# Cross-attention of a decoder block: weights multiplied with the memory once, ahead of the blocks, instead of query, score and value products in every block; six weight slots

## The chip, the cores and the metric

One core of a Trainium2 chip runs the whole step as one program. The metric is device time in microseconds (us) of one execution. Three runs of the kernel before gave 2971.23, 2973.12 and 2975.67 us, median 2973.12. Names: PE is TensorE, DVE VectorE, ACT ScalarE, POOL GpSimd, SP SyncE.

## The reference

The step has 2048 prompt tokens and 8 decode tokens (one each of 8 sequences), all of width 1024. In the order of the reference, with everything in 32-bit floats:

```
h = h + hybrid_mixer(rmsnorm(h, g_mix))              # gated conv and mLSTM, w_in, w_out
kk, vv = split(rmsnorm(mem, g_mem) @ w_xkv)          # 256 memory rows, 4 heads of 256
q = rmsnorm(h, g_cross) @ w_xq                       # per head:
p = softmax(q @ kk.T * 256**-0.5)
h = h + concat(p @ vv) @ w_xo
h = h + (silu(g) * u) @ w_down                       # g, u = split(rmsnorm(h, g_ffn) @ w_gu)
y = rmsnorm(h, g_final)
```

The prompt tokens attend to the 256 new memory rows, which are the same for all of them; each decode token attends to its own cached keys and values (`cache_mem_k`, `cache_mem_v`). The keys and values of the new memory are outputs too.

## The kernel before, in words

Activations are kept with the feature on the partition: a tile holds 8 slices of 128 features, and tokens run along the columns. The 2048 prompt tokens are worked in 5 blocks of 512, 384, 384, 384 and 384 tokens (`BLK`); a block goes through the mixer, the cross-attention and the FFN before the next one begins. The 8 decode columns ride along as columns 385 to 392: in the mixer of block 1 (`DM`), in the output product and the queries of block 2 (`DO`), and in the attention output and the FFN of block 3 (`DX`).

A product with a weight is made of "groups": one group is 128 output features, 8 slices of input, and three passes for each slice (high part of the weight with high and low part of the activation, low part of the weight with the high part), so 24 matmuls of as many columns as the block has tokens; `gemm`, line 518. A group's weight is one tile of 128 by 1024. It needs two forms, high and low (`w_hl`, a slot of 1 MB), of which there are `NS = 5` slots. In a program there are first 16 groups for keys and values (`G_KV`) on 256 columns, then 5 times 121 groups: gate 1, sigmoid gates 4, heads 24, output 8 (`O_OUT`), queries 8 (`O_XQ`), attention output 8 (`O_XO`), FFN 68.

Weights of the first 16 groups and of block 0 arrive unsplit: SP loads 512 KB into one of `NR = 2` raw slots (line 326), ACT copies the high part (`w_high`, line 823), and the low part is subtracted by DVE (first 16 groups, line 1175) or POOL (block 0, line 419); only then SP loads the next weight into that raw slot. In block 0 SP also stores the split weight (line 341), and blocks 1 to 4 load it as 1 MB, split (line 348). `w_high` of a group stands in ACT's program behind the group `NS` before it, and ACT, like every engine, works its program in order.

While the last keys and values are made, ACT, DVE and PE also normalise and split the tokens of block 0 (`next_scale`, `next_high`, `next_low`, lines 1164, 840, 1170). In block 0 the values are turned by 16 transposes (`turn_mem`, line 552).

The cross-attention of a block: 8 query groups; behind them, in hooks of the groups, for each of 4 heads the scores (line 682: per 128 tokens 6 matmuls of 256 columns), the maxima (DVE, 1439), the exponentials (ACT, 1011), the division (DVE, 1450), transposes of the probabilities (692), and the product with the values in plain 32-bit floats (699); its result is split (1023, 1455) and goes into the 8 groups of attention output. The decode tokens' queries are kept (`dqd`), turned and stored (`turn_q`, line 722), and DVE works on the cached keys and values piece by piece during the FFN of block 2 (`dec_piece`); the result goes as 8 columns through the attention output of block 3.

## Time and profile before

| | |
|---|---|
| median of 3 runs | 2973.12 us |
| the profiled execution | 2972.26 us, its span 2970.5 us (1.8 us lie around the span) |
| PE busy | 2921.0 us, 98% of the span |
| DVE, ACT, POOL busy | 1212.2, 761.0, 379.7 us |
| granted TensorE clock over the span | 0.996 of full speed |
| moved by DMA | 776 MB, 261 GB/s |

"Busy" is the time in which at least one instruction of an engine runs. The distance between the starts of two matmuls, not the duration of one, is what a matmul costs on a busy PE, since they overlap. A matmul of plain 32-bit floats stands in the trace as two records.

### The profile page before, as it was taken

Reading aid. Unit: us, or ns where it says so; the run is one execution under the profiler, and the core shown is the slowest. Engines: PE = TensorE matmul, PEld = TensorE weight load, DVE = VectorE, ACT = ScalarE, POOL = GpSimd, SP = SyncE. Lnnn points to the kernel's source line nnn. Section 1 sums busy time; section 2 is a strip of 40 time slices with the busy share of each in tenths; the row PEclk is TensorE's granted clock in tenths of the full one; section 3 lists DMA queues with packets and bytes.
Section 4 is the critical chain, followed back from the end, with each engine's and each line's share of the span. In section 5 each row is a group of like instructions: output and inputs, shape, how many; then the busy total and the mean of one; then the engine's idle time right before and its main releaser. Section 6 shows DMA issues by size and latency. Waiting matters only on the chain.

```text
span 2970.5 us, 39232 instructions
## 1 busy us (share of the span) xinstructions
PE 2921.0 (98%) x16162; PEld 2759.7 (93%) x16162; DVE 1212.2 (41%) x2337; ACT 761.0 (26%) x1510; POOL 379.7 (13%) x252
## 2 busy tenths in 40 slices
PE   7899999999999999999999999999999999999998
PEld 6788778888899999999999999999999999999998
DVE  6455554224624444233344546334422243442223
ACT  4443443232332220113232011322311032231001
POOL 0443434444210000000000111000000000000000
PEclk9999999999999999999999999999999999999999
DMA  5876858788876488777667989866467777646675
GB/s 190 321 269 225 282 203 298 277 277 309 300 274 244 162 324 305 264 264 285 219 226 273 338 321 372 308 226 249 174 241 260 260 268 266 229 179 248 254 268 195
DMA packets 126585, 776.02 MB, mean 261 GB/s; under 512 B 14885, under 2 KB 18405, under 8 KB 46665
## 3 DMA queue, kind: packets, MB, share of 16 engines
q1 hardware_dynamic: 109744, 710.71, 66.0%
q0 software_dynamic: 13904, 59.48, 5.8%
q10 hardware_dynamic: 2760, 3.33, 0.4%
q8 instruction: 129, 2.11, 0.3%
q14 instruction: 48, 0.39, 0.0%
HBM read 633.52 MB, written 139.94 MB: 260 GB/s over the span
## 4 chain that ended last, share of the span: by engine, by line
PE 90%; DMA 4%; DVE 2%; ACT 2%; POOL 1%; issue 1%; SPq 0%; DVEq 0%; ACTq 0%
PE gb L518 83%; DMA w_raw<-w_st 2%; PE ta L682 2%; DMA w_hl<-split_d 1%; POOL w_hl L419 1%; PE td L699 1%; PE tb L699 1%; ACT w_hl L823 1%; DMA w_raw<-w_kv 1%; PE ta L603 0%; PE tb L572 0%; DVE w_hl L1175 0%; PE ta L526 0%; PE tb L614 0%; PE td L621 0%
## 5 line engine op out<-in xcount | busy, mean ns | idle before, releaser
L518 PE MATMUL gb<-xn_hi,w_hl 128*128 128x384 f32 (+2 forms) x6440 | 1770.4, 350 | 14.2 <-DVE xn_lo L1170 7.7
L518 PEld LDWEIGHTS gb<-xn_hi,w_hl 128*128 128x128 f32 x6440 | 1178.7, 188 | 73.2 <-DVE xn_lo L1170 8.8
L518 PE MATMUL gb<-xn_lo,w_hl 128*128 128x384 f32 (+2 forms) x3240 | 1123.1, 347 | 0.0
L518 PE MATMUL gb<-act_hi,w_hl 128*128 128x384 f32 (+3 forms) x3296 | 872.4, 344 | 18.4 <-DVE w_hl L1175 10.6
L518 PEld LDWEIGHTS gb<-act_hi,w_hl 128*128 128x128 f32 x3296 | 598.8, 189 | 46.3 <-DVE w_hl L1175 10.9
L518 PEld LDWEIGHTS gb<-xn_lo,w_hl 128*128 128x128 f32 x3240 | 609.5, 188 | 28.7 <-issue 1.2
L518 PE MATMUL gb<-act_lo,w_hl 128*128 128x384 f32 (+3 forms) x1648 | 563.9, 342 | 0.0
L1218 DVE TENSOR_TENSOR work<-gb,r_res 128x384 f32<-128x384 f32 (+2 forms) x260 | 151.8, 585 | 652.0 <-PE gb L518 588.1
L419 POOL TENSOR_TENSOR w_hl<-w_raw,w_hl 128x1024 fp32r<-128x1024 f32 x120 | 292.4, 2440 | 413.7 <-ACT w_hl L823 413.7
L518 PEld LDWEIGHTS gb<-act_lo,w_hl 128*128 128x128 f32 x1648 | 311.6, 189 | 13.6 <-issue 0.7
L1410 DVE TENSOR_TENSOR x<-x,gb 128x384 f32<-128x384 f32 (+2 forms) x200 | 115.4, 581 | 373.2 <-PE gb L518 369.9
L823 ACT ACTIVATE w_hl<-w_raw 128x1024 fp32r<-128x1024 f32 x132 | 138.9, 1057 | 329.6 <-DMA w_raw<-w_st 158.4
L1080 ACT ACTIVATE work<-work 128x384 f32<-128x384 f32 (+2 forms) x110 | 59.9, 545 | 504.1 <-DVE work L1218 504.0
L1083 ACT ACTIVATE act_hi<-work 128x384 fp32r<-128x384 f32 (+2 forms) x110 | 60.1, 546 | 346.2 <-DVE work L1637 346.2
L997 ACT ACTIVATE work<-x 128x384 f32<-128x384 f32 (+2 forms) x120 | 65.6, 546 | 270.0 <-DVE x L1410 249.7
L1420 DVE TENSOR_TENSOR r_res<-r_res,work 128x384 f32<-128x384 f32 (+2 forms) x120 | 94.5, 787 | 68.6 <-ACT work L997 67.2
L1637 DVE TENSOR_TENSOR work<-work 128x384 f32<-128x384 f32 (+2 forms) x110 | 87.4, 794 | 35.2 <-ACT work L1080 24.0
L382 POOL DMA_DIRECT2D big<-rows_d x20 | 10.9, 550 | 675.1 <-DMA rows_d<-big 675.1
L887 ACT ACTIVATE big<-gb,cst 128x384 f32<-128x384 f32 (+1 forms) x80 | 48.5, 607 | 186.6 <-PE gb L518 186.0
L1320 DVE TENSOR_TENSOR work<-ta,big 128x128 f32<-128x128 f32 x64 | 18.7, 292 | 186.8 <-ACT work L968 144.4
L1624 DVE TENSOR_TENSOR act_lo<-work,act_hi 128x384 fp32r<-128x384 f32 (+2 forms) x110 | 85.6, 778 | 12.5 <-ACT act_hi L1083 11.8
L1423 DVE SCALAR_TENSOR_TENSOR xn_lo<-x,cst,xn_hi 128x384 fp32r<-128x384 f32 (+2 forms) x80 | 55.8, 698 | 0.0
(248 smaller groups left out, 1806.9 us busy)
## 6 DMA issues: line engine op xcount, KB each, us to landing
w_hl<-split_d SPq DMA_DIRECT2D x484, 1024.0 KB, 5.2
split_d<-w_hl SPq DMA_DIRECT2D x121, 1024.0 KB, 5.0
w_raw<-w_st SPq DMA_DIRECT2D x121, 512.0 KB, 6.0
w_raw<-w_kv SPq DMA_DIRECT2D x16, 512.0 KB, 3.6
big<-kd_d POOLq DMA_DIRECT2D x8, 1024.0 KB, 9.0
big<-vd_d POOLq DMA_DIRECT2D x8, 1024.0 KB, 11.3
x<-x_blk POOLq DMA_DIRECT2D x8, 768.0 KB, 8.0
big<-x_blk POOLq DMA_DIRECT2D x6, 768.0 KB, 6.0
```

The lines of the kernel that those rows point to most:

```text
L419: pool.tensor_tensor(lo_w, raw_w, hi_w.bitcast(F32), ALU.subtract).then_inc(w_lo_done, 1)
L518: mm = pe.matmul(gb[:, ps, 0:wd], a[:, s, k * P:(k + 1) * P], r[:, k, 0:wd], start=(first and k == ks[0] and i == 0), stop=(last and k == ...
L682: mm = pe.matmul(ta[:, t // 2, (t % 2) * 256:(t % 2) * 256 + 256], a[:, kt, t * P:(t + 1) * P], r[:, kt, :], start=(dt == 0 and i == 0), s ...
L823: act.activation(w_hi[:, n % NS, :], w_raw[:, n % NR, :], ACT.Copy).then_inc(w_hi_done, 1)
L997: act.activation(sq_res[:, 0:wd], x[:, e, 0:wd], ACT.Square).then_inc(res_sq, 1)
L1080: act.activation(et[:, 0:W], gt[:, 0:W], ACT.Silu).then_inc(e_ffn, 1)
L1083: act.activation(act_hi[:, f, 0:W], ht[:, 0:W], ACT.Copy).then_inc(hid_hi, 1)
L1218: return lambda ps: v.tensor_tensor(dst[:, 0:wd], ps[:, 0:wd], r_res[:, 0:wd], ALU.mult)
L1410: return lambda ps: v.tensor_tensor(x[:, e, 0:wd], x[:, e, 0:wd], ps[:, 0:wd], ALU.add)
L1420: v.tensor_tensor(acc_res[:, 0:wd], acc_res[:, 0:wd], sq_res[:, 0:wd], ALU.add).then_inc(res_acc, 1)
L1624: v.tensor_tensor(act_lo[:, f, 0:W], ht[:, 0:W], act_hi[:, f, 0:W].bitcast(F32), ALU.subtract).then_inc(hid_lo, 1)
L1637: v.tensor_tensor(ht[:, 0:W], et[:, 0:W], ut[:, 0:W], ALU.mult).then_inc(h_ffn, 1)
```

## The change

Since `q @ kk.T` is `xn @ (w_xq @ kk.T)`, and `(p @ vv) @ w_xo` is `p @ (vv @ w_xo)`, the products in the inner brackets don't depend on the token. The change makes them once, between the 16 key and value groups and block 0: 16 more weights are loaded raw (`w_xq` turned, `w_xo`; `G_KV` goes from 16 to 32, `G_MEM = 16` keeps the old count), and 32 products of 128 by 512 come out: four for each of the 4 heads of `w_xq` (48 matmuls of 256 columns a head) and of `w_xo` (24 of 512). ACT and DVE copy them in turn into one of 8 places of 256 KB (`made`), ACT's queue stores them to `made_d`, and block 0 loads them from there like raw weights (16 of 512 KB) and splits them.

In each block the eight query groups become two runs of `wide`: the token slice is the stationary side, the made weight streams with 512 columns (two heads' 256 memory rows), and the scores come out at once. The probabilities, turned and split, go into the groups of attention output directly. Score products, value products, queries and `turn_mem` are gone. The norm of the tokens enters as a factor of the exponential, by columns (`sum_cols`, `norm_cols`).

The decode tokens can't use the made weights. In the attention output of block 2 their queries are made by 16 products of plain 32-bit floats (8 rows by 512 columns) with `w_xq`, unsplit, loaded by POOL's queue into 4 places (`dwt`); in the output groups of block 3 their attention output by 16 more with `w_xo`, and 8 small matmuls that turn it. The split of block 0's tokens moves from the last key and value groups into the new stretch, `NS` is 6, and the next tokens of block 1 are loaded some groups earlier.

```
-G_KV = 16
+G_MEM = 16
+G_KV = 32
+NPRE = 32
-NS = 5
+NS = 6
...
+            for h in range(HEADS):
+                pe.wait_ge(mem_lo, 2 * h + 2)
+                for j in range(4):
+                    bank = pre_bank(i)
+                    for n in range(2):
+                        for dt in range(2):
+                            if j == 0 and n == 0:
+                                slot_ready(g)
+                            for f, (a, r) in enumerate([(w_hi, act_hi), (w_hi, act_lo), (w_lo, act_hi)]):
+                                mm = pe.matmul(bank[:, n * NMEM:(n + 1) * NMEM], a[:, g % NS, c:c + P], r[:, 2 * h + dt, NMEM:2 * NMEM], ...
...
+            for i in range(NPRE):
+                if i % 2 == 0:
+                    pre_made(act, i)
+                    after(act, pre_stored[i % 8], 16 * (i // 8))
+                    act.activation(made[:, i % 8, :], gb[:, (G_MEM + i) % NP, :], ACT.Copy).then_inc(pre_a, 1)
+                if i:
+                    store_made(i - 1)
+                if i % 4 == 3:
+                    w_high(G_MEM + i // 4 * 2)
+                    w_high(G_MEM + i // 4 * 2 + 1)
+                if i < KT:
+                    read_out(act, G_MEM - 1)
+                    act.activation(act_hi[:, i, 0:NMEM], vfeat[:, i, :], ACT.Copy).then_inc(mem_hi, 1)
+                elif i < 2 * KT:
+                    next_high(0, i - KT)
...
-                opening(gw(b, O_XQ), W, 0)
-                q_hooks = {3: {3: lambda: scores(0)}, 4: {6: lambda: ptrans(0)}, 5: {2: lambda: scores(1) or pv(0)},
...
+                wide(0, {(1, CH - 1): sum_cols})
+                if b == 0:
+                    wide(1, {(1, 3): lambda: ptrans(0, 0), (2, 1): lambda: ptrans(0, 1), (2, 3): lambda: ptrans(1, 0),
+                             (3, 1): lambda: ptrans(1, 1)})
+                else:
+                    wide(1, {(1, 2): lambda: ptrans(0, 0) or ptrans(0, 1), (2, 2): lambda: ptrans(1, 0) or ptrans(1, 1)})
...
                 xo(0, 0)
                 xo(1, 0)
-                ptrans(2)
-                scores(3)
-                pv(2)
                 xo(2, 0)
                 xo(0, 1)
+                ptrans(2, 0)
+                ptrans(2, 1)
...
+                    if b == DO and m < 7:
+                        hooks = {3: lambda: decode_queries(m)}
+                    gemm(gw(b, O_XO + m), TOK, act_hi, act_lo, hooks=hooks)
```

`wide` itself, as it stands in the changed kernel:

```
def wide(p, hooks):
    for q in range(4):
        g = gw(b, O_XQ) + 4 * p + q
        slot_ready(g)
        for t in range(CH):                       # CH: 128-token slices of the block
            for n in range(2):
                kt = 2 * q + n
                for f, (a, r) in enumerate([(xn_hi, w_hi), (xn_lo, w_hi), (xn_hi, w_lo)]):
                    mm = pe.matmul(score_bank(p, t), a[:, kt, t * P:(t + 1) * P], r[:, g % NS, n * 512:n * 512 + 512], ...
```

How the instructions move on PE, in block 1 where the scores of the second head and the values of the first stood. Before (`act_hi` and `act_lo` hold the queries, `mem_k` the keys, `big` the turned probabilities, `mem_v` the values):

```order
L682 MATMUL ta<-mem_k_hi,act_hi 128x256
L682 MATMUL ta<-mem_k_hi,act_lo 128x256
L682 MATMUL ta<-mem_k_lo,act_hi 128x256
L699 MATMUL td<-big,mem_v 128x384 [waits pt_evac]
L699 MATMUL td<-big,mem_v 128x384
L699 MATMUL tb<-big,mem_v 128x384 x2
L518 MATMUL gb<-xn_hi,w_hl 128x384
L518 MATMUL gb<-xn_lo,w_hl 128x384
```

And PE in the changed kernel, block 1, in the second run of `wide` (`td` and `ta` are score banks, `w_hl` holds the made weights, `work` the probabilities, `gm` and `tb` take them turned):

```order
L843 MATMUL td<-w_hl,xn_lo 128x512
L843 MATMUL td<-w_hl,xn_hi 128x512
L825 MATMUL gm<-mats,work 128x128 [waits o_lo,p_done]
L825 MATMUL gm<-mats,work 128x128 x2
L825 MATMUL tb<-mats,work 128x128 [waits o_lo,p_done]
L825 MATMUL tb<-mats,work 128x128 x2
L843 MATMUL ta<-w_hl,xn_hi 128x512 [waits split_loaded_4]
L843 MATMUL ta<-w_hl,xn_lo 128x512
```

Only transposes are left between the streams of 512 columns; the two kinds of products at L682 and L699 are gone.

ACT behind the last key and value group, before (line 823 is `w_high`, 840 the high part of block 0's tokens, 873 that of the keys, 892 the gates of block 0):

```order
L823 ACTIVATE w_hl<-w_raw 128x1024 [waits group_done,w_loaded_0]
L840 ACTIVATE xn_hi<-big 128x512 [waits mix_scaled]
L873 ACTIVATE mem_k_hi<-x 128x256 [waits out_v] x2
L823 ACTIVATE w_hl<-w_raw 128x1024 [waits group_done,w_loaded_1]
L840 ACTIVATE xn_hi<-big 128x512 [waits mix_scaled]
L873 ACTIVATE mem_k_hi<-x 128x256 [waits out_v] x2
L823 ACTIVATE w_hl<-w_raw 128x1024 [waits group_done,w_loaded_0]
L873 ACTIVATE mem_k_hi<-x 128x256 [waits out_v] x2
L892 ACTIVATE big<-gb,cst 128x512 [waits group_done]
```

And ACT in the new stretch of the changed kernel, the sixth of its eight heads (984 is `w_high`, 1069 the copy of a made product into its place, 1063 a store of one):

```order
L1069 ACTIVATE big<-gb 128x512 [waits pre_stored_4,pre_done]
L1063 DMA made_d<-big 128x4x128 [waits pre_v]
L1063 DMA made_d<-big 128x4x128 [waits pre_a]
L1069 ACTIVATE big<-gb 128x512 [waits pre_stored_6,pre_done]
L1063 DMA made_d<-big 128x4x128 [waits pre_v]
L1063 DMA made_d<-big 128x4x128 [waits pre_a]
L984 ACTIVATE w_hl<-w_raw 128x1024 [waits group_done,w_loaded_0]
L984 ACTIVATE w_hl<-w_raw 128x1024 [waits group_done,w_loaded_1]
L1069 ACTIVATE big<-gb 128x512 [waits pre_stored_0,pre_done]
```

Each head ends with two `w_high`, and the copy that frees PE's bank for the next head's products stands behind both.

## Rows read from the trace of the kernel before

**Rows 1.** First part of the page: busy time, share of the span, instructions.
```profile
PE 2921.0 (98%) x16162; PEld 2759.7 (93%) x16162; DVE 1212.2 (41%) x2337; ACT 761.0 (26%) x1510; POOL 379.7 (13%) x252
```
**Rows 2.** Waits of PE: waiter, releaser, total us, times, longest.
```profile
PE gb L518 <- DVE xn_lo L1170: 7.7, 2, 7.3
...
PE ta L682 <- DVE act_lo L1465: 1.7, 1, 1.7
```
**Rows 3.** Timeline of PE, attention of block 1: start, us, instruction.
```profile
1001.31 0.51 PE L518 MATMUL gb<-xn_hi,w_hl 128*128 128x384 f32 x2
...
1007.03 0.34 PE L518 MATMUL gb<-xn_hi,w_hl 128*128 128x384 f32 x1
...
1008.10 0.28 PE L682 MATMUL ta<-mem_k_lo,act_hi 128*128 128x256 f32 x1
...
1009.88 0.28 PE L682 MATMUL ta<-mem_k_lo,act_hi 128*128 128x256 f32 x1
```
**Rows 4.** Timeline of PE, value products, block 0 (512) and block 1 (384).
```profile
354.55 1.88 PE L699 MATMUL td<-big,mem_v 128*128 128x512 f32 x4
356.27 1.88 PE L699 MATMUL tb<-big,mem_v 128*128 128x512 f32 x4
...
1012.61 1.45 PE L699 MATMUL td<-big,mem_v 128*128 128x384 f32 x4
1013.90 1.45 PE L699 MATMUL tb<-big,mem_v 128*128 128x384 f32 x4
```
**Rows 5.** Chain that ended last, pieces in order of time: start, us, what.
```profile
26.92 2.88 PE gb L518 x24
...
94.65 5.47 PE gb L518 x24
...
194.42 2.42 POOL w_hl L419
197.22 6.09 DMA w_raw<-w_st
204.52 2.41 POOL w_hl L419
```
**Rows 6.** Timeline of PE, end of the value groups, first gate group.
```profile
72.41 0.28 PE L518 MATMUL gb<-act_hi,w_hl 128*128 128x256 f32 x1
74.93 0.47 PE L518 MATMUL gb<-xn_hi,w_hl 128*128 128x512 f32 x1 [2.24 <-issue]
...
85.21 0.80 PE L518 MATMUL gb<-xn_hi,w_hl 128*128 128x512 f32 x1 [7.28 <-DVE xn_lo L1170]
```
**Rows 7.** Busy time by window: PE, PEld, DVE, ACT, POOL, clock, DMA share, GB/s.
```profile
85.20:90.80 5.60, 5.20 (x11) 3.64 (x12) 4.05 (x6) 2.24 (x4) 2.38 (x1) 0.50 0.95 357
```
**Rows 8.** DMA from 0 to 9 us: packets, MB, share; issues, KB, us to landing.
```profile
q10 hardware_dynamic: 759, 0.74, 30.4%
...
x<-mem_x ACTq DMA_DIRECT2D x4, 256.0 KB, 8.2
```
**Rows 9.** DMA from 40 to 60 us, the same columns.
```profile
q1 hardware_dynamic: 936, 3.44, 53.5%
...
w_raw<-w_kv SPq DMA_DIRECT2D x6, 512.0 KB, 3.2
```
**Rows 10.** Instructions that touch the raw slots: duration min/median/max in ns.
```profile
L823 ACT ACTIVATE w_hl<-w_raw x132: 1041/1060/1067, 29.8 to 781.7; 128x1024 fp32r<-128x1024 f32 x132
...
L419 POOL TENSOR_TENSOR w_hl<-w_raw,w_hl x120: 2345/2397/3179, 71.1 to 782.8; 128x1024 fp32r<-128x1024 f32 x120
```
**Rows 11.** Instructions of the softmax lines, the same columns.
```profile
L1011 ACT ACTIVATE work<-ta,work x64: 456/471/477, 341.7 to 2646.7; 128x256 f32<-128x256 f32 x64
L1011 ACT ACTIVATION_READ_ACCUMULATOR work<-ta,work x64: 192/198/212, 342.1 to 2647.0; 128x1 f32 x64
...
L1439 DVE TENSOR_REDUCE work<-ta x40: 417/685/695, 339.4 to 2645.6; 128x2 f32<-128x512 f32 x24, 128x1 f32<-128x256 f32 x16
...
L1450 DVE TENSOR_SCALAR work<-work x64: 352/353/357, 345.7 to 2650.2; 128x256 f32<-128x256 f32 x64
```

More of the change, by code:

```diff
@@ new lines, in _ @@
+            for h in range(HEADS):
+                pe.wait_ge(mem_lo, KT + 2 * h + 2)
+                for j in range(4):
+                    i = HEADS * 4 + h * 4 + j
+                    bank = pre_bank(i)
+                    mt, half = j // 2, j % 2
+                    for dt in range(2):
+                        g = G_MEM + KT + 2 * h + dt
+                        if j == 0:
+                            slot_ready(g)
+                        for f, (a, r) in enumerate([(act_hi, w_hi), (act_lo, w_hi), (act_hi, w_lo)]):
+                            mm = pe.matmul(bank, a[:, 2 * h + dt, mt * P:(mt + 1) * P], r[:, g % NS, half * 512:half * 512 + 512],
+                                           start=(dt == 0 and f == 0), stop=(dt == 1 and f == 2))
+                    if j < 3:
+                        mm.then_inc(pre_done, 1)
+                    else:
+                        mm.then_inc(group_done, 2)
@@ new lines, in score_bank, with prob_high @@
+                def score_bank(p, t):
+                    if p == 0:
+                        return gb[:, (gw(b, O_XQ) + t) % NP, :] if t < NP else gm[:, :]
+                    return (ta[:, 0, :], ta[:, 1, :], td[:, :], tb[:, :])[t]
+                def prob_high(h):
+                    for mt in range(MT):
+                        act.wait_ge(pt_done, pt0 + 2 * h + mt + 1)
+                        bank = gm if b == 0 and h < 2 else (gm, tb)[mt]
+                        act.activation(act_hi[:, 2 * h + mt, 0:TOK], bank[:, 0:TOK], ACT.Copy).then_inc(o_hi, 1)
```

576 lines of the change are left out of this document (334 added, 242 removed).

## The prediction

> **What bounds the kernel now.** I read the page's first part, then PE's waits, then the timeline of PE in one attention, then the chain in order of time at the start. PE is busy for 2921.0 of 2970.5 us [rows 1], and its waits are small: the longest is 7.3 us for the low part of block 0's tokens, the score products waited 1.7 us in all [rows 2]. So the kernel is as long as the sum of PE's matmuls, and a change is worth the matmuls that it takes away, less the ones that it adds, less new idle time. What a matmul costs is the distance of two starts: 34 matmuls of 384 columns from 1001.31 to 1007.03 are 33 steps of 0.173 us; 16 of 256 columns from 1008.10 to 1009.88 are 15 steps of 0.119 us [rows 3]; 24 of 512 take 5.47 us, 0.228 each [rows 5]. Plain 32-bit products are dearer: 4 records, which are 2 matmuls of 512 columns, take 356.27 - 354.55 = 1.72 us, so 0.86 us each; with 384 columns 1.29 us for two [rows 4].
>
> There is one place where PE doesn't set the time: a raw weight's way. A raw slot is held for landing, high part on ACT (1.06 us), low part on POOL (2.40 us) [rows 10]. In the chain one turn of a slot goes from 194.42 to 204.52, 10.1 us, of which 6.09 us is a landing beside other traffic [rows 5]. Two slots give two weights in 10.1 us. In block 0 a group lasts 5.47 us, so this just holds.
>
> **The change part by part.** All sums are on the profiled execution, 2972.3 us, which is 0.9 us under the median of the runs.
>
> Taken from PE. Scores: 16 slices of 128 tokens x 4 heads x 6 matmuls = 384 x 0.119 = 45.6 us. Value products: 8 pairs in block 0 at 1.72 and 32 in the others at 1.29 = 13.8 + 41.3 = 55.0 us. Sixteen transposes of the values: no row of theirs stands here; a matmul of 256 columns takes 0.119, so at most 1.9 us, I take 1.4. Queries: a 384-token block goes from 192 matmuls of 0.173 to 144 of 0.228, 33.3 to 32.8 us, four times 0.5 = 2.0; the 8 decode columns leave two sets of 192 matmuls, 1.4 us by columns (twice 8/384 of 33.3). Together 105.4.
>
> Added to PE. The made weights: 192 x 0.119 + 96 x 0.228 = 22.8 + 21.9 = 44.7 us. The decode products: 2 x 16 matmuls of 512 columns in plain floats at 0.86 = 27.5 us, and some 1.2 us for the small ones that turn them. Together 73.4. The sums of squares by columns take the place of a wide plain product, about even. PE alone: 105.4 - 73.4 = 32.0 us less.
>
> The new stretch. Its eight heads need PE for 44.7 / 8 = 5.6 us each, and two raw weights each. Since POOL makes the low part now (2.40 us; before, for keys and values, it was DVE), the slots set the pace P of a head. From below: landing 3.2 us when little else moves [rows 9], 1.06, 2.40 and 0.5 of hand-over, 7.1 us. From above 10.1 [rows 5]. Six weight slots do not help out: `w_high` of two weights stands behind each head in ACT's program, and behind those the copy that frees PE's bank. When a load is late ACT waits, the copy behind it waits, and PE runs out of its three banks after three more products (4.2 us). So the lead that the slots could give is not used, P binds from the second head on.
>
> Between 7.1 and 10.1 DMA decides. A packet of about 1 KB cost 0.304 x 16 x 9 us / 759 = 58 ns [rows 8], one of 3.7 KB 0.535 x 16 x 20 / 936 = 183 ns [rows 9]; the line through both gives 36 ns at 512 B. In the first four heads a store has 256 packets of 1 KB, in the last four 512 of 512 B. Four stores a head are 3.7 and 4.6 us of 16 engines, two loads 3.3 us: 7.0 and 7.9 us of DMA per head, which at P = 9 is 80 to 90% busy. Landing is then near the loaded value, and I take P = 9. Taking the first and the last head at PE's pace, the stretch is 2 x 5.7 + 6 x 9 = 65.4 us, 20.7 longer than its matmuls (9.3 at P = 7.1, 27.3 at 10.1).
>
> What goes at the start. Between the last value group (72.41) and 85.21 PE did only 12 matmuls of the gate group (2.7 us): 12.8 - 2.7 - 0.3 = 9.8 us idle [rows 6]. It waited for the low part of block 0's tokens, behind ACT, which waited for weights. After that PE ran for 5.6 us at a granted clock of 0.50, the lower level of 1.2 GHz [rows 7]; about 2.9 us of this is loss. Splitting the tokens lies inside the new stretch now, beside matmuls: 12.7 us come back. If the clock drops in the new stretch (PE is idle for a third there), a head takes up to 11 us of PE instead of 5.6, but the clock comes up again once PE is filled; this is in the upper half of the range.
>
> The attention. Scores of a slice come every 6 x 0.228 = 1.37 us; ACT needs 2 x (0.47 + 0.20) = 1.34 us, DVE 0.69 for the maxima, 2 x 0.35 to divide [rows 11]. They just keep up. For the first two heads the second `wide` covers the tail. For the last two, after the last score it is some 0.7 + 0.3 + 1.34 + 0.9 + 0.4 = 3.6 us until the transposes can start, and PE has 4 pieces of 6 matmuls, 4.2 us. That holds with little to spare: I take 0.2 us a block. In block 0 a `w_high` stands between the scores and their exponentials on ACT; all eight exponentials (5.4 us) begin after it, against 5.5 us of cover: 3 us. The wait of 1.7 us goes. Decode: loads for the products have two groups (some 15 us) from the freeing of their place, no landing of 512 KB here is that long, 1 us for the rest. Together +3.3, from -1.7 to +12.
>
> The rest: POOL gets 16 more weights, all in the new stretch. Queries no longer need DVE; nothing waited for that. The later start of the cached keys lies under FFN groups, and PE has three banks, 12 us, before a late DVE stops it.
>
> Sum: -32.0 + 20.7 - 12.7 + 3.3 = -20.7 us. 2972.3 - 20.7 + 0.9 = 2952.5, I say 2952 us.
>
> **A rule of the Trainium skill.** The four loads of 256 KB on ACT's queue at the start, which all went out at once, landed at a median of 8.2 us [rows 8]: if they share the time evenly, one takes 2.05 us, and if two and a half have landed by the median, 3.3. The Trainium skill, "DMA: Bandwidth & Descriptors", section "Bandwidth", calls for transfers of at least 1 MiB, and its section "Anatomy of one DMA — SWDGE (gpsimd) path" fits one DMA by about 2.0 us plus bytes over 436 GB/s (for POOL's path), an estimate of 2.6 us for one of our stores, 83 us for 32 of them if one waited for the other. By that rule the result is rival A. The row's 2.05 us would make 66 us, no more than my stretch; no row shows a store of this size, so the trace neither bears the rule out nor denies it.
>
> **The rivals.**
> A. The stores queue up one behind the other. At 2.7 us each (between 2.05 and 3.3) 32 take 86 us; the stretch is as long, 20.6 more than I say, and the time is 2973: no change. For it: all are in one queue, and a place is used again after 8 products. Against it: loads of 512 KB land in 3.2 us [rows 9], so a DMA's fixed part overlaps with others.
> B. Small writes are dear, and the change makes the kernel slower. No store of 512 B or 1 KB pieces to memory stands in the trace, only reads. If a packet costs twice the row, 115 ns, the 12288 packets take 88 us and the 16 loads 16 x 1.63 = 26: 114 us, 49 more than I say: 3001 us. It decides from 86 us of DMA on, which is (86 - 26) x 16 / 12288 = 78 ns a packet.
> C. The stretch runs at PE's pace: P = 7.1 or less because the stores don't get in the way, and the attention without stalls: 2952 - 11.4 - 3 = 2938 us. For it: DMA share 0.54 and landing of 3.2 us beside the loads of keys and values [rows 9]. Against it: ACT's program order, above.
> D. The gain ends in the attention. If the 3.6 us chain is 3 us longer and the second turn of transposes waits 2 us, it is 5 us in each of 5 blocks: 2977 us with block 0. Against it: in the kernel before the same chain ran beside PE with almost no wait [rows 2].
>
> **How the numbers follow.** My forecast (2944 to 2962, P from 7.7 to 10.5) gets 0.44; C 0.22; A 0.09; B 0.08; D 0.06; milder forms of A and D, between 2962 and 2967, 0.11. What a measurement can tell from no change is 0.2%, 6 us, so faster is under 2967 and slower over 2979. Faster: 0.44 + 0.22 + 0.11 = 0.77. A and most of D are "same", 0.13; B and the rest of D "slower", 0.10. The range: below, PE's own sum with P = 7.1 and no stall is 2952 - 11.4 - 5 = 2936; above, P = 10.1 (+6.6) and the worst attention (+8.7) are 2967, and it reaches into A: 2974. The forecast's own range is 2944 to 2962.
>
> **What would show it.** Right: in the profile after, no line for scores on `mem_k` or products with `mem_v`; 288 matmuls that make the weights; between the last value group and the first gate group some 60 to 70 us, PE busy for two thirds, ACT's waits in it for the raw weights; blocks 1 to 4 each about 19 us shorter (scores 8.5, values 10.3, queries 0.5), of which blocks 2 and 3 give back 14 each. Wrong: a stretch over 86 us (ACT waiting for `made` places says A or B, by the packet time of ACT's queue) or under 55 (C); waits of PE for probabilities over 2 us a block (D); a decode product at another pace than 0.86 us, or PE at the lower clock for long.

## The result: slower, 2989.5 us where 2952 were forecast

The changed kernel takes 2989.47 us (median of 4 runs, 2987.12 to 2991.16), the kernel before 2972.18 (4 runs, 2970.31 to 2975.67): ratio 1.0061, 95% interval 1.0047 to 1.0074. The forecast was a gain of 21 us, the result is a loss of 17, 15 us above the end of the range.

The first part of the page after, which answers to [rows 1]:

```profile
PE 2912.0 (97%) x15801; PEld 2720.9 (91%) x15801; DVE 1181.5 (40%) x2243; ACT 752.9 (25%) x1470; POOL 425.5 (14%) x284
```

PE is busy for 9 us less, not 32 (part of the missing 23 is matmuls at a lower clock, which keep PE busy for longer: the granted clock over the span is 0.990, before 0.996), and the span is 18.8 us longer. The waits of PE after (waiter, releaser, total us, times, longest), against [rows 2]:

```profile
PE gb L599 <- DVE w_hl L1375: 11.2, 2, 9.4
PE gb L664 <- ACT big L1069: 9.8, 3, 5.4
PE gb L599 <- DVE act_lo L1350: 8.1, 4, 4.5
PE gb L843 <- DVE x L1617: 5.8, 2, 4.4
PE gb L646 <- issue: 5.1, 2, 3.5
...
PE gm L825 <- DVE work L1676: 3.2, 1, 3.2
```

L646 and L664 make the weights in the new stretch, L843 is `wide`, L825 turns the probabilities. All of these waits lie at the start, in the stretch and in block 0. The step at which ACT reads the gates of a block cuts the trace into pieces:

| | forecast | measured | off by |
|---|---|---|---|
| first made product (before: last value group at 72.4) | 72.4 | 78.1 | +5.7 |
| new stretch, first made product to first gate matmul | 65.4 | 78.3 | +12.9 |
| from there to the gates read | 3.4 | 8.0 | +4.6 |
| block 0, gates to gates, against 711.1 before | -25.3 | -8.9 | +16.4 |
| blocks 1 to 4 and the end, against 2170.9 before | -48.1 | -48.1 | 0.0 |

The forecast's column is its own terms: for block 0 scores 11.4, values 13.8 and transposes 1.4 go, 1.3 of stalls come; the last row is what is left of -20.7. The errors add up to 39.6 us, all ahead of block 1.

The three places in the trace after. At the start ACT splits a sixth weight inside the loop over the memory slices, and waits for its load (timeline: start, us, instruction, idle time before it and what ended it):

```profile
25.75 1.06 ACT L1030 ACTIVATE w_hl<-w_raw 128x1024 fp32r<-128x1024 f32 x1 [4.43 <-DMA w_raw<-w_kv]
...
32.67 0.47 ACT L1008 ACTIVATE work<-td,cst 128x256 f32<-128x256 f32 x1 [2.91 <-PE td L607]
```

The second row is the first scale factor, at 26.96 before. In the stretch PE is busy for 55.8 of 78.3 us (windows: PE, PEld, DVE, ACT, POOL, clock, DMA share, GB/s), and the gate group behind it runs at a mean granted clock of 0.74, part of it on the lower level:

```profile
78.10:117.00 38.90, 27.23 (x192) 26.30 (x192) 32.88 (x34) 19.20 (x32) 21.79 (x9) 0.90 0.63 211
117.00:156.40 39.40, 28.60 (x96) 21.74 (x97) 8.66 (x13) 14.53 (x19) 20.06 (x9) 0.80 0.88 293
156.40:164.40 8.00, 7.99 (x27) 6.43 (x28) 0.78 (x2) 1.44 (x2) 2.38 (x1) 0.74 1.03 382
```

ACT in the last heads: each `w_high` (L984) waits for its raw weight, the copy of a product (L1069) stands behind two of them, and the reading of the gates (L1099) behind another. Then SP's issues, where a 1 MB store (L387) goes out right ahead of each raw load (L372):

```profile
138.15 1.06 ACT L984 ACTIVATE w_hl<-w_raw 128x1024 fp32r<-128x1024 f32 x1 [2.98 <-DMA w_raw<-w_st]
...
145.53 1.06 ACT L984 ACTIVATE w_hl<-w_raw 128x1024 fp32r<-128x1024 f32 x1 [4.74 <-DMA w_raw<-w_st]
150.91 1.06 ACT L984 ACTIVATE w_hl<-w_raw 128x1024 fp32r<-128x1024 f32 x1 [4.32 <-DMA w_raw<-w_st]
...
151.87 0.58 ACT L1069 ACTIVATE big<-gb 128x512 f32<-128x512 f32 x1
...
163.44 1.06 ACT L984 ACTIVATE w_hl<-w_raw 128x1024 fp32r<-128x1024 f32 x1 [6.56 <-DMA w_raw<-w_st]
164.40 0.67 ACT L1099 ACTIVATE big<-gb,cst 128x512 f32<-128x512 f32 x1
```
```profile
141.69 0.33 SPq L387 DMA_DIRECT2D split_d<-w_hl  x1
142.05 1.68 SPq L372 DMA_DIRECT2D w_raw<-w_st  x1
149.04 0.33 SPq L387 DMA_DIRECT2D split_d<-w_hl  x1
149.41 0.45 SPq L372 DMA_DIRECT2D w_raw<-w_st  x1
```

In block 0's attention PE waited for its banks at the start of `wide`, for the first turned probabilities of the second pair of heads, and for a low part:

```profile
396.73 0.50 PE L843 MATMUL gb<-w_hl,xn_hi 128*128 128x512 f32 x1 [1.40 <-DVE x L1617]
402.75 0.67 PE L843 MATMUL gb<-w_hl,xn_hi 128*128 128x512 f32 x1 [4.36 <-DVE x L1617]
...
457.05 0.69 PE L825 MATMUL gm<-mats,work 128*128 128x128 f32 x4 [3.22 <-DVE work L1676]
...
505.22 0.72 PE L599 MATMUL gb<-xn_hi,w_hl 128*128 128x512 f32 x1 [2.38 <-DVE xn_lo L1632]
```

### The profile page after: what moved, and what is told of

Read it like the earlier page. It is cut to its first block, busy times and chain, and to the rows that moved or that the text cites. A ratio compares the mean times of both kernels' runs of the same rounds, so it can differ in the third digit from the quotient of the medians.

```text
span 2989.3 us, 38462 instructions
## 1 busy us (share of the span) xinstructions
PE 2912.0 (97%) x15801; PEld 2720.9 (91%) x15801; DVE 1181.5 (40%) x2243; ACT 752.9 (25%) x1470; POOL 425.5 (14%) x284
## 3 DMA queue, kind: packets, MB, share of 16 engines
q10 hardware_dynamic: 15504, 11.72, 1.3%
## 4 chain that ended last, share of the span: by engine, by line
PE 86%; DMA 6%; DVE 2%; POOL 2%; ACT 2%; issue 1%; SPq 0%; ACTq 0%; DVEq 0%
PE gb L599 75%; DMA w_raw<-w_st 3%; PE gb L843 3%; POOL w_hl L475 2%; PE ta L843 2%; DMA w_raw<-w_kv 2%; ACT w_hl L984 1%; PE td L843 1%; DMA big<-kd_d 1%; DMA w_hl<-split_d 1%; DMA w_raw<-made_d 0%; PE ta L712 0%; PE tb L687 0%; PE gm L825 0%; PE tb L723 0%
## 5 line engine op out<-in xcount | busy, mean ns | idle before, releaser
L599 PE MATMUL gb<-xn_hi,w_hl 128*128 128x384 f32 (+2 forms) x5800 | 1589.7, 350 | 6.6 <-DVE xn_lo L1632 2.4
L599 PEld LDWEIGHTS gb<-xn_hi,w_hl 128*128 128x128 f32 x5800 | 1063.5, 188 | 57.0 <-issue 4.8
L599 PE MATMUL gb<-xn_lo,w_hl 128*128 128x384 f32 (+2 forms) x2920 | 1014.3, 347 | 0.0
L599 PEld LDWEIGHTS gb<-xn_lo,w_hl 128*128 128x128 f32 x2920 | 550.6, 189 | 24.7 <-issue 0.5
L475 POOL TENSOR_TENSOR w_hl<-w_raw,w_hl 128x1024 fp32r<-128x1024 f32 x136 | 330.3, 2434 | 497.3 <-ACT w_hl L984 497.2
L1426 DVE TENSOR_TENSOR work<-gb,r_res 128x384 f32<-128x384 f32 (+2 forms) x220 | 128.3, 585 | 549.4 <-PE gb L599 513.9
L984 ACT ACTIVATE w_hl<-w_raw 128x1024 fp32r<-128x1024 f32 x147 | 154.6, 1058 | 380.5 <-DMA w_raw<-w_st 171.0
L1629 DVE TENSOR_TENSOR r_res<-r_res,work 128x384 f32<-128x384 f32 (+2 forms) x120 | 90.3, 753 | 71.3 <-ACT work L1203 69.9
L436 POOL DMA_DIRECT2D big<-rows_d x20 | 10.9, 551 | 659.6 <-DMA rows_d<-big 659.6
L843 PE MATMUL gb<-w_hl,xn_hi 128*128 128x512 f32 x240 | 77.9, 397 | 5.8 <-DVE x L1617 5.8
## 6 DMA issues: line engine op xcount, KB each, us to landing
big<-kd_d POOLq DMA_DIRECT2D x8, 1024.0 KB, 11.7
big<-vd_d POOLq DMA_DIRECT2D x8, 1024.0 KB, 12.8
```

The costliest lines, as they stand in the source:

```text
L475: pool.tensor_tensor(lo_w, raw_w, hi_w.bitcast(F32), ALU.subtract).then_inc(w_lo_done, 1)
L599: mm = pe.matmul(gb[:, ps, 0:wd], a[:, s, k * P:(k + 1) * P], r[:, k, 0:wd], start=(first and k == ks[0] and i == 0), stop=(last and k == ...
L843: mm = pe.matmul(score_bank(p, t), a[:, kt, t * P:(t + 1) * P], r[:, g % NS, n * 512:n * 512 + 512], start=(kt == 0 and f == 0), stop=(kt ...
L984: act.activation(w_hi[:, n % NS, :], w_raw[:, i % NR, :], ACT.Copy).then_inc(w_hi_done, 1)
L1426: return lambda ps: v.tensor_tensor(dst[:, 0:wd], ps[:, 0:wd], r_res[:, 0:wd], ALU.mult)
L1629: v.tensor_tensor(acc_res[:, 0:wd], acc_res[:, 0:wd], sq_res[:, 0:wd], ALU.add).then_inc(res_acc, 1)
```

## The experiments

Theory: PE's own sums are right, and the loss is made by the way of the raw weights (two raw slots, loads behind 1 MB stores, ACT's program order) and by the sixth weight at the start. Rivals: DVE beside POOL's low parts; small packets; the loss is not the change's. Each kernel was timed 4 to 11 times beside the kernel before, whose median lay between 2971.1 and 2971.7 us; ratios are to it, with 95% intervals. The results of all runs, with the pieces read from one trace of each (us):

| kernel | first made product | gates of block 0 read | block 0 | blocks 1 to 3 | median | ratio |
|---|---|---|---|---|---|---|
| before | | 88.5 | 711.1 | 1625.6 | 2971.5 | 1 |
| changed | 78.1 | 164.4 | 702.2 | 1596.7 | 2989.5 | 1.0061 |
| 1 five weights at start | 72.9 | 158.9 | 698.9 | 1595.2 | 2981.5 | 1.0037 |
| 2 low parts on DVE | 76.0 | 164.5 | 701.7 | 1596.4 | 2990.3 | 1.0064 |
| 3 roundings apart | 77.5 | 169.1 | 700.7 | 1596.8 | 2995.2 | 1.0078 |
| 4 load first | 78.4 | 158.2 | 689.1 | 1596.7 | 2974.0 | 1.0009 |
| 5 five split slots | 71.6 | 156.9 | 696.1 | 1599.3 | 2981.3 | 1.0032 |
| 6 before, load first | | 85.2 | 703.4 | 1625.1 | 2961.3 | 0.9966 |
| 7 runs 1, 4 and two orders | 72.2 | 153.9 | 680.1 | 1597.1 | 2959.8 | 0.9959 |
| 8 five split, four raw, load first | 69.3 | 136.4 | 683.1 | 1600.5 | 2948.1 | 0.9924 |
| 9 six split, four raw, load first | 69.9 | 145.2 | 681.3 | 1597.5 | 2950.6 | 0.9933 |
| 10 run 9, stores held back | 70.2 | 132.1 | 682.2 | 1595.9 | 2938.6 | 0.9889 |
| 11 products in 2 KB rows | 77.8 | 162.5 | 703.5 | 1596.0 | 2987.9 | 1.0055 |
| 12 run 8, old order, without the two | 69.8 | 140.1 | 685.6 | 1599.8 | 2954.5 | 0.9944 |
| 13 run 10, low parts on DVE | 69.6 | 128.7 | 683.4 | 1595.4 | 2935.6 | 0.9880 |
| 14 run 10, tokens split later | 68.1 | 126.3 | 683.2 | 1595.2 | 2933.8 | 0.9876 |
| 15 runs 13 and 14 | 69.0 | 125.8 | 681.7 | 1596.0 | 2933.4 | 0.9874 |

**1. Five weights split at the start.**

```
-                if k < NS:
+                if k < NS - 1:
                     act.wait_ge(w_loaded...)          # DVE's low part likewise
...
+            k = NS - 1                                # behind the loop, ahead of rnorm
+            act.activation(w_hi[:, k, :], w_raw[:, k % NR, :], ACT.Copy)
```

> The changed kernel with one edit: six slots stay, but only five weights are split in the loop over the memory's slices; the sixth is split behind that loop, ahead of the first scale factor. Theory (the sixth weight in the start loop costs the 5.7 us by which the first scale factor comes later, 32.67 against 26.96 us): the scale factor at about 27 us, the gate of block 0 some 5 to 6 us earlier, the kernel at 1.0042 of the kernel before in place of 1.0061. Rival (the lateness is given back in the 46 us of key and value products that follow, or the sixth weight is late there instead): the gate moves by under 2 us, ratio 1.0055 to 1.0061.

Measured: 1.0037 (1.0024 to 1.0049). The gates are read 5.5 us earlier and block 0 is 3.3 shorter. The sixth weight in the loop makes 5.2 of the first 5.7 us (72.9 against 78.1), and nothing gives it back. Why block 0 is shorter too was not followed.

**2. Low parts on DVE.**

```
-            for g in range(G_MEM, G_LOW):             # POOL's low parts
+            for g in range(G_KV, G_LOW):
...
-                if g + NS < G_MEM:                    # DVE, first 16 groups
-                    w_low(g + NS)
+                w_low(g + NS)
...
+                n = G_MEM + NS + (i // 4 - 1) * 2     # DVE, product i
+                if i > 3 and i % 4 == 0 and n < G_KV:
+                    w_low(n)
+                    w_low(n + 1)
```

> The changed kernel with one edit: the low parts of the 16 weights that feed the made products are taken by VectorE (where the low parts of the first 16 are taken) and no longer by GpSimd. Theory (beside a GpSimd low part of 2.4 us each VectorE instruction takes 2.4 to 2.9 us in place of 0.4 to 0.75, and VectorE's copies of the products come late by that): no VectorE instruction of the stretch over 1.5 us, heads 1 to 4 go from 9.2 us each towards 8 or below, the stretch of 78.3 us is 4 to 8 us shorter, ratio 1.0035 to 1.0048. Rival (the loads and stores set the pace, VectorE only waits elsewhere): stretch within 2 us of 78.3, ratio 1.0055 to 1.0066.

Measured: 1.0064 (1.0052 to 1.0077), no gain. DVE in the first four heads, grouped by shape (count, busy us, mean ns, idle before), changed kernel and this one:

```profile
L1364 DVE SCALAR_TENSOR_TENSOR big<-big,cst,r_mix 128x512 f32<-128x512 f32 x8 | 10.2, 1273 | 0.0
L1400 DVE TENSOR_TENSOR act_lo<-x,act_hi 128x256 fp32r<-128x256 f32 x3 | 7.2, 2386 | 1.9 <-ACT act_hi L1050 1.9
```
```profile
L1373 DVE TENSOR_TENSOR w_hl<-w_raw,w_hl 128x1024 fp32r<-128x1024 f32 x8 | 9.5, 1220 | 2.3 <-ACT w_hl L982 2.3
L1362 DVE SCALAR_TENSOR_TENSOR big<-big,cst,r_mix 128x512 f32<-128x512 f32 x8 | 6.0, 745 | 0.0
...
L1397 DVE TENSOR_TENSOR act_lo<-x,act_hi 128x256 fp32r<-128x256 f32 x3 | 1.3, 418 | 0.0
```

The effect on DVE is as I said (0.42 us in place of 2.39 for the same subtraction, 0.75 in place of 1.27), but it was not what set the time. The stretch begins 2.1 us earlier and the gates are read no earlier: from first copy to first copy heads 2 to 4 take 10.9, 10.5 and 11.1 us, in the changed kernel 9.5, 9.4 and 9.2. So with two raw slots relieving DVE alone gains nothing. That the raw weights' turn takes it back is the likely reason, since the same edit gains 3 us with four raw slots (run 13); the low parts' new place in DVE's order was not tested by itself.

**3. The two roundings apart.**

```
-                if i % 4 == 3:
-                    w_high(G_MEM + i // 4 * 2)
-                    w_high(G_MEM + i // 4 * 2 + 1)
+                if i > 3 and i % 2 == 0:
+                    w_high(G_MEM + (i // 4 - 1) * 2 + i % 4 // 2)
```

> The changed kernel with one edit: ScalarE's two roundings of a next pair of weights no longer stand together behind the third product of a head, ahead of its copy of the next head's first product; one stands behind that copy and one behind the next. Theory (ScalarE's copy is late because it stands behind roundings that wait for loads; TensorE waited 9.8 us for those copies): TensorE's waits for the copies fall under 4 us, the stretch is 4 to 6 us shorter, ratio 1.0040 to 1.0048. Rival (the weights themselves land too late, so the wait moves from the copy to the low parts): the copies are in time, TensorE waits as long for w_hl, stretch within 2 us, ratio 1.0055 to 1.0066.

Measured: 1.0078 (1.0066 to 1.0091), slower than both expected. The gates are read 4.7 us later. PE's waits for ACT's copies fall from 9.8 to 6.6 us, where under 4 was expected. A rounding taken later leaves its raw slot full for longer, so that the next load can only start later; this is argued from the program and was not followed in the trace. It speaks for the slots, and against an order on ACT that needs only to be mended.

**4. The load ahead of the store.**

```
-                    keep(g)                           # waits for the low part, stores 1 MB
+                    sp.wait_ge(w_lo_done, RAW[g] - G_MEM)
                 if i < len(raws):
                     weights(raws[i])
+                if g >= G_KV:
+                    keep(g)
```

> The changed kernel with one edit: where SyncE stores a split weight of 1 MB and then loads the next raw weight, the load is issued first. Theory (from 138 us on the raw loads of the last heads stand behind 1 MB stores and land late; ScalarE waited 1.2 to 6.6 us each for them): the last four heads lose 4 to 8 us of their 39, block 0 may gain a little as well, ratio 1.0030 to 1.0048. Rival (the transfers are at the rate that the memory gives, 0.88 of the DMA engines' time, so order changes nothing, or the stores that come later hold up the slots): ratio 1.0055 to 1.0075.

Measured: 1.0009 (1.0000 to 1.0019), 15.5 us less than the changed kernel by the medians, more than the theory said; between the profiled runs 19.4, of which 6.2 to the gates and 13.1 in block 0. ACT's waits for raw weights from 170 to 690 us, in the changed kernel and here; the third row is the largest of `w_high` in run 12, where no row for raw weights is over 2 us:

```profile
ACT w_hl L984 <- DMA w_raw<-w_st: 95.3, 29, 7.8
```
```profile
ACT w_hl L985 <- DMA w_raw<-w_st: 61.5, 22, 6.5
```
```profile
ACT w_hl L984 <- PE gb L599: 146.4, 40, 10.8
```

29 waits become 22; with four raw slots ACT waits for PE and no more for raw weights. PE's wait at the start of `wide` goes from 5.8 to 2.9 us here, and in run 12 to none, though both leave the order there as it was.

**5. Five split slots.** `NS = 6` becomes `NS = 5`, with one semaphore less in two lists.

> The changed kernel with five weight slots, as the kernel before has them, in place of six; all else as changed. Theory (the sixth slot costs its weight at the start and gives nothing back, since what waits is the raw loads behind it): first scale factor at about 27 us, gate of block 0 5 to 6 us earlier, block 0 within 4 us of 702, ratio 1.0035 to 1.0045, as with five weights split at the start. Rival (the sixth slot is needed: the score products hold four weights open, the made products two, and with five slots fewer weights are ready ahead): block 0 over 706 us or the stretch longer, ratio 1.0055 to 1.008.

Measured: 1.0032 (1.0019 to 1.0044). Without the sixth slot 8 us are gained, as in run 1, which keeps the slot and only splits its weight later; without it blocks 1 to 3 are 2.6 us longer.

**6. The kernel before, load first.** The edit of run 4 in the kernel before.

> The kernel before, with one edit: SyncE issues the load of the next raw weight ahead of the 1 MB store of a split weight, as in the run of the changed kernel that gained 15.5 us by it (6.2 to the gate, 13 in block 0). Theory (the changed kernel made that order dear: its stretch leaves the loads late when block 0 starts, TensorE is slowed by idle gaps, and the loads never catch up; before, the loads were in time): under 3 us gained, ratio 0.999 to 1.0005. Rival (the order costs block 0 in any kernel, and the gain has nothing to do with the change): block 0 goes from 711 to about 700 us, ratio 0.9950 to 0.9970.

Measured: 0.9966 (0.9953 to 0.9978). The rival holds: 10 us go in the kernel before too, 7.7 of them in block 0. So of the 15.5 us of run 4, 10 were not the change's doing. My sentence that two raw slots "just hold" in block 0 was wrong already of the kernel before.

**7. Three edits together.** Those of runs 1 and 4, and in block 0:

```
-                    elif e >= 3:
+                    elif b == 0 and use == 0 and e >= 6:
+                        if e == 6:
+                            evac(g, add_x(6, new))
+                            evac(g + 1, add_x(7, new))
+                    elif e >= 3:
...
-                w_high(gw(b, O_XQ + 7))
                 exps(1)
+                w_high(gw(b, O_XQ + 7))
```

> The changed kernel with three edits: five weights split in the start loop (the sixth behind it), the raw load ahead of the store, and in block 0 two orders: VectorE takes the sums of the last two output groups directly one behind the other, and ScalarE's second group of exponentials stands ahead of its rounding of the last score weight. Theory (the losses at the start, in the stretch and in block 0's attention are separate): the gate at 152 to 154 us, block 0 at 682 to 686, TensorE's waits at the start of the score products (2.9) and for the turned probabilities (3.2) under 2 us together, ratio 0.9965 to 0.9985. Rival (the stretch takes back what the start gains, since loads pace it, and in block 0 loads do the same): ratio 1.000 to 1.0015.

Measured: 0.9959 (0.9946 to 0.9973), 29.7 us below the changed kernel. PE's waits from 150 to 834 us:

```profile
PE tb L724 <- DVE work L1533: 2.5, 1, 2.5
PE ta L711 <- ACT big L1098: 1.5, 1, 1.5
PE gm L826 <- DVE work L1685: 0.8, 1, 0.8
```

The 5.8 us ahead of `wide` are gone (2.9 in run 4, without the two orders) and 3.2 are 0.8; block 0 is 680.1. The two orders were not run alone.

**8. Five split and four raw slots.** `NS = 5`, `NR = 4` (the same room in memory), load first, the two orders.

> The changed kernel with the raw load ahead of the store, the two orders of block 0, and the 8 KB per partition of the sixth split slot given to raw weights: five split slots and four raw slots in place of six and two. Theory (in the stretch the two raw slots set the pace: a load waits until the low part of the weight two before is taken, so loads, roundings and copies follow one another head by head): the stretch goes from 72 to 56 to 62 us, ScalarE's waits for raw weights in it fall under 1 us each but in the last heads, ratio 0.9915 to 0.9945. Rival (the transfers themselves are at the memory's rate, 0.88 to 0.9 of the DMA engines' time in the stretch's second half, and more slots only queue more): the stretch at 68 to 74 us, ratio 0.9965 to 0.999.

Measured: 0.9924 (0.9912 to 0.9937). The gates are read at 136.4: 17.5 us before run 7. The raw slots set the pace. What comes last now is the stores of the products; ACT at the end of the stretch (ACTq is its queue, L1064 the issue of a store), and the window 113 to 150:

```profile
126.73 1.06 ACT L985 ACTIVATE w_hl<-w_raw 128x1024 fp32r<-128x1024 f32 x1 [1.24 <-PE gb L665]
127.45 8.85 ACTq L1064 DMA_DIRECT2D made_d<-big  x1
127.70 1.04 ACT L985 ACTIVATE w_hl<-w_raw 128x1024 fp32r<-128x1024 f32 x1
136.35 0.69 ACT L1100 ACTIVATE big<-gb,cst 128x512 f32<-128x512 f32 x1 [7.61 <-issue]
...
156.47 0.69 ACT L1095 ACTIVATE big<-gb,cst 128x512 f32<-128x512 f32 x1 [16.65 <-DMA made_d<-big]
```
```profile
113.00:150.00 37.00, 33.44 (x147) 27.05 (x145) 12.13 (x20) 12.20 (x16) 20.17 (x10) 1.00 1.05 384
```

One issue took 8.85 us, and the gates (L1100) stood behind it. The sigmoid gates (L1095) then waited 16.65 us for the stores to land, as the program makes them; it is for this instruction that PE waited 9.9 us. All DMA engines are in use. This is a part of rival A, which appears once the loads no longer set the pace.

**9. Six split and four raw slots.** Run 7's edits, and two more raw slots, cut from the decode weights' buffer:

```
-        w_raw = sb("w_raw", [P, NR, D])
+        w_raw = sb("w_raw", [P, 6, D])
-        dwt = sb("dwt", [P, 4, D])
+        dwt = w_raw[:, 2:6, :]
```

> Six split slots and four raw slots (the two more are cut from the decode weights' buffer, which is free until block 1), five weights split in the start loop, the raw load ahead of the store, and the two orders of block 0. Theory (raw slots set the pace of the stretch, and the sixth split slot is worth the 3 to 4 us by which blocks 2 and 3 were shorter with it): gate of block 0 at 135 to 138 us, blocks 1 to 4 as in the changed kernel, 2940 to 2945 us, ratio 0.9895 to 0.9915. Rival (the sixth slot gives nothing once the raw slots are there): 2946 to 2952 us, as with five split slots and four raw ones, ratio 0.9915 to 0.9935.

Measured: 0.9933 (0.9920 to 0.9945); the rival's bounds hold, for another reason. Blocks 1 to 3 are 3.0 us shorter than in run 8, as the theory said, but the gates are read 8.8 us later. The 1 MB stores of split weights begin at 119.6 us, 122.4 in run 8, and in the window 113 to 150 the products' stores take a median of 15.2 us to land, 7.3 in run 8; PE waits 5.2 us for a copy and 10.2 for the sigmoid gates. That the 1 MB stores are the cause is what run 10 tests.

**10. The first 1 MB stores held back.** On run 9:

```
+                if g == G_KV + 3:
+                    for slot_stored in pre_stored:
+                        sp.wait_ge(slot_stored, 16 * (NPRE // 8))
+                    for j in range(4):
+                        keep(G_KV + j)
+                elif g > G_KV + 3:
                     keep(g)
```

> As the kernel with six split and four raw slots, and the 1 MB stores of block 0's first four split weights wait until the made products' stores have landed. Theory (with four raw slots the made products' stores are what comes last: TensorE waited 9.9 us behind ScalarE, which waited 7.6 us for them to land, beside 1 MB stores at 384 GB/s): that wait falls under 4 us, block 0's loads do not suffer, 4 to 8 us below the kernel without it. Rival (the megabytes only move: block 0 starts with 4 MB more to store and its loads wait): the wait goes, and block 0 gets longer by as much, within 2 us of the kernel without it.

Measured: 0.9889 (0.9875 to 0.9902), 12.1 us below run 9, more than the theory said, and block 0 is 0.9 longer. First the window 113 to 150, then ACT at block 0's first `w_high`:

```profile
113.00:150.00 37.00, 36.01 (x159) 29.51 (x158) 9.87 (x13) 14.84 (x20) 23.00 (x11) 1.00 1.00 354
```
```profile
143.61 1.06 ACT L990 ACTIVATE w_hl<-w_raw 128x1024 fp32r<-128x1024 f32 x1 [10.84 <-DMA split_d<-w_hl]
```

PE is busy for 36.0 of the 37 us, 33.4 in run 8, and its waits for the products' stores are gone. The wait moved as the rival said: ACT now waits 10.84 us for a split weight's store. But PE does not wait for ACT there for long (1.9 and 2.4 us in the whole start of block 0).

**11. Products stored in rows of 2 KB**, in the wrong places, so the attention's output is another.

```
+                dst = made_d[i // 2][:, i % 2 * 512:i % 2 * 512 + 512]
+                src = made[:, i % 8, :]
```

> The changed kernel with one edit that makes its output another: each made product is stored as it lies, in rows of 2 KB, and not cut into rows of 1 KB and 512 B at the places where the weights want them (the same bytes, the wrong places). Theory (the products' stores cost what their bytes cost, some 40 ns a packet in the page of the changed kernel): stretch within 3 us of 78.3, ratio 1.0045 to 1.0070. Rival (small packets are dear and crowd out the raw loads, which pace the stretch): stretch 8 us shorter or more, ratio under 1.0035.

Measured: 1.0055 (1.0041 to 1.0069); the gates are read 1.9 us earlier, and first products to gates take 1.6 us less. ACT's queue in the two pages (packets, MB, share of 16 engines), changed kernel and this one:

```profile
q10 hardware_dynamic: 15504, 11.72, 1.3%
```
```profile
q10 hardware_dynamic: 7312, 11.72, 1.1%
```

0.013 x 16 x 2989.3 / 15504 = 40 ns a packet, and 8192 packets fewer save 0.2% of the span, 6 us of all engines. Small packets cost little: rival B falls.

**12. Run 8's slots with the old order.** `NS = 5`, `NR = 4`, nothing else.

> The changed kernel with five split slots and four raw slots in place of six and two, and SyncE's old order: the store of 1 MB ahead of the raw load. Theory (two raw slots pace the stretch, and with four the loads are far enough ahead that the order of load and store matters less): the stretch at 62 to 68 us, block 0 at 684 to 692, ratio 0.9930 to 0.9965. Rival (it is the order that counts, and four raw slots gave their 17 us only behind it): stretch over 70 us, block 0 over 695, ratio 0.9985 to 1.0030.

Measured: 0.9944 (0.9931 to 0.9956), as the theory said. Two raw slots more are worth 26.8 us against run 5 (16.8 to the gates, 10.5 in block 0). The order, which gave 15.5 us with two raw slots, gives 6.4 with four, together with the two orders of block 0 (run 8 against this run).

**13 to 15. What paces the first heads.** With four raw slots heads 2 to 4 still took 9.5, 9.4 and 8.8 us from first copy to first copy, the later ones 5.4 to 5.7. Run 13 is the edit of run 2 on run 10. Run 14 moves the splitting of block 0's tokens, where DVE has time:

```
-                    next_scale(0, i)                  # DVE, products 0 to 7
-                elif i < 2 * KT:
-                    next_low(0, i - KT)
+                elif 12 <= i < 20:
+                    next_scale(0, i - 12)
+                elif 20 <= i < 28:                    # ACT's next_high likewise
+                    next_low(0, i - 20)
```

Run 15 does both.

> The fastest kernel so far (run with the stores held back), with the low parts of the 16 weights of the made products on VectorE in place of GpSimd, as in the earlier run that gained nothing with two raw slots. Theory (with four raw slots VectorE is what paces heads 2 to 4: each of its instructions beside a GpSimd low part takes 2.4 to 2.9 us): heads 2 to 4 go from 9.5, 9.4 and 8.8 to 7 to 8 us, gates read 3 to 6 us earlier than 132.1, ratio 0.9870 to 0.9880. Rival (VectorE only changes what it waits with, since 16 subtractions of 1.2 us are as much work for it; or the clock sets the pace): gates within 2 us of 132, ratio 0.9883 to 0.9895.

> The fastest kernel so far, with the scaling and splitting of block 0's tokens moved by three heads: scaling beside products 12 to 19, high and low parts beside products 20 to 27, where VectorE was idle for three quarters of the time. Theory (VectorE's work in heads 1 to 4 delays the copies): heads 2 to 4 at 6 to 7.5 us, later heads at 5.7 still, gates read 4 to 8 us earlier than 132.1, ratio 0.9860 to 0.9877. Rival (the work is late at its new place, and the gate group waits for the low part of the tokens as it did in the kernel before): the heads are faster, and the gate group begins later by as much, ratio 0.9883 to 0.9900.

> Both edits: the low parts of the made products' weights on VectorE, and the splitting of the tokens three heads later. Theory (one cause, VectorE's time in the first four heads): heads 2 to 4 at 5.7 to 6.5 us, near TensorE's pace, gates read at 122 to 127 us, ratio 0.9845 to 0.9870. Rival (the gains are the same ones, and what is left in these heads is loads): no more than the better of the two alone, within 1.5 us.

Measured: 0.9880 (0.9866 to 0.9895), 0.9876 (0.9861 to 0.9890), 0.9874 (0.9858 to 0.9891). The gates are read 3.4, 5.8 and 6.3 us earlier than in run 10; by the medians 3.0, 4.7 and 5.2 us are gained, which the intervals of the ratios do not separate. The first heads in run 10 and run 14, same window:

```profile
69.30:100.00 30.70, 26.41 (x197) 26.02 (x197) 26.56 (x30) 17.31 (x29) 17.01 (x8) 0.89 0.67 222
```
```profile
69.30:100.00 30.70, 28.04 (x208) 26.16 (x206) 24.55 (x24) 16.91 (x28) 22.63 (x9) 1.00 0.84 276
```

Heads 2 to 4 go to 8.6, 8.4 and 8.5 us in run 13, less than the theory said, to 8.3, 5.4 and 4.9 in run 14 and to 7.8, 6.7 and 5.6 in run 15. The granted clock of the window is 0.94 in run 13 and 1.00 in the other two, 0.89 in run 10, so a part of the gain is the clock. By these traces, one of each kernel, DVE paced the heads once the loads didn't. The two edits together gave no more than the better one, as the rival had it: heads 5 to 7 of run 14, which got DVE's work, take 9.3, 6.5 and 7.2 us.

## Why the prediction was wrong

**PE's sums held.** Blocks 1 to 4 are 48.1 us shorter, as forecast to 0.1. Blocks 2 and 3, which have the decode products, go from 543.4 and 543.1 to 537.1 and 540.0, blocks 1 and 4 lose 19.5 and 19.3: 13 and 16 us for decode products where 14 was said. The plain products came at the price taken from [rows 4]. No wait of PE for probabilities stands in these blocks, so rival D falls there.

**The failed step** is the one on the raw slots, in its two places. In "The new stretch" I took six heads at P = 9 and the first and the last at PE's pace, 65.4 us. Six distances between the heads' first copies are 7.7, 9.5, 9.4, 9.2, 9.5 and 8.5 us, 53.8 together where 54 was said. It was the ends that failed. The seventh is 12.8, not 5.7: there a 1 MB store goes ahead of each load, and my sum of DMA per head (7.0 and 7.9 us) left these stores out. With the load first it is 9.4 (run 4), with four raw slots 5.5 even in the old order (run 12). What is left at the two ends takes 11.7, not 5.7; of this 7.1 lie ahead of the first copy, where run 12 has 1.7. That the six came out at 9 is in part luck, for the reason that I gave holds only for the later ones. With four raw slots the last three distances are at PE's pace (5.4 to 5.7), in the old order too (runs 10 and 12), so those were bound by slots; heads 2 to 4 still took about 9 us, and needed DVE relieved as well (runs 13 to 15), of which I had said nothing.

In the second place, "What bounds the kernel", I read from one turn of 10.1 us against two groups of 5.47 that it "just holds" in block 0 [rows 5]. It does not hold: ACT waited 95.3 us for raw weights between 170 and 690 us, and with two more raw slots and nothing else block 0 is 10.5 us shorter (run 12 against run 5), of the 16.4 by which the forecast was off. The 5.8 us for the three banks at the start of `wide`, which I had not seen either, belong to the same fault: they are gone in run 12. The other 6.1 us between the changed kernel and run 12 came with five split slots (run 5), and why they did stays open. The kernel before had the same fault for 7.7 us (run 6), which PE's table of waits did not show as one row: it came as small waits for whatever the late weight held up, 6.0 us in three rows, of which run 6 has none.

**The terms that were missing or mis-sized beside it.** Splitting the sixth weight in the start loop had no price: 5.2 us at the start, 8 in all by run 1. The 12.7 us that the old gate group should give back were 8.1. The stretch now ends in long waits and the gate group runs at the lower level for a part (mean clock 0.74 against 0.50 in [rows 7]; in runs 8 and 10 the clock from 126 to 140 us is 1.00), and ACT reads the gates some 2 us after the group's end, behind a `w_high` that waited 6.56 us for its raw weight. The 12.7 were too many besides: they leave 3.4 us for the gate group, whose 16 matmuls take 3.6 at 0.228. In block 0's attention I allowed 3 us for `w_high` ahead of the exponentials, and that was right (3.2).

**The rivals.** A: the stretch was not the 86 us of stores in a row; PE waited for the stores only in runs 8, 9 and 12. The Trainium skill, "DMA: Bandwidth & Descriptors", section "Anatomy of one DMA — SWDGE (gpsimd) path", gives a fit for one DMA, and my estimate from it of 83 us was for 32 stores one after the other. This case does not bear out that they go so: in run 10 all 32 went out while the products took 57 us, with a median of 4.1 us from issue to landing, so they overlap. B fell by run 11. C, the stretch at PE's pace, did not hold for the change as it was made; with other slots and orders run 10 came to C's 2938 and run 15 below it, by other gains too (the order of run 6 is worth 10 us without the change).

What part of the gain is the change's: run 15, the fastest, stands 28 us below run 6, which is the kernel before with the one order that helped it too. What four raw slots would be worth in the kernel before was not tried, so the change's own part may be smaller. Why the sixth split slot makes blocks 1 to 3 shorter by 3 us was not followed up.

## What to carry to other kernels

Before a new stage is priced by its matmuls, follow one weight through its buffers: slots in flight divided by the turn of a slot is a rate, and if the stage wants more, memory for another landing slot is worth more than for another finished one (here two raw slots gave 27 us, and a sixth split slot as it was filled lost 8). In a queue that both stores results and fetches what is needed next, issue the fetch first, and hold back bulk stores that nobody waits for while small stores that somebody waits for are out. And look at the waits of the engines that feed the full one: 115.4 us of ACT's waits for loads stood in the trace before (100 to 640 us), where PE's own table showed nothing over 3.4 us in block 0. Such a sum is a question and not yet a loss: in run 6 62.6 us of it are left in the same window, and PE has no wait in block 0.

## What was not expected of the hardware

A DVE subtraction of 128x256 that ran beside a POOL subtraction of 128x1024 took 2.39 us in place of 0.42, about the POOL instruction's own time [rows 10]; when DVE did all of them itself, each of those of 128x1024 took 1.22 us. The issue of one store on ACT's queue took 8.85 us in run 8, 9.15 in run 12 and 10.63 in run 9, where the DMA engines were full (share 1.04 to 1.05 from 113 to 150 us), against 0.37 us for the last store of run 10, and the gates behind it on ACT were read only when it had ended. The window of run 8 moved 384 GB/s at its share of 1.05.
